# Pair rows of six tiles read whole during the last four expert blocks, with a masked second gather for the late rows

## The chip, the cores and the metric

One core of a Trainium2 chip runs the kernel. The metric is the device time of one execution in microseconds. The kernel before took 610.31 us (median of three runs, 609.31 to 610.9).

## The reference, cut to what matters

One decoder layer over 1024 prompt tokens and 64 sample tokens of width 1024. Four mixers and an output projection give `x`; the part around the change is the mixture of experts and the last norm:

```
expert(token)   = the two best of 8 experts in the best of 4 groups      # 32 experts, F = 128
out(token, k)   = silu(h @ w_gate[e_k]) * (h @ w_up[e_k]) @ w_down[e_k]  # k = 0, 1
x(token)        = x + gate_0 * out(token, 0) + gate_1 * out(token, 1)
y(token)        = rmsnorm(x, g_final)
```

## The kernel before, in words

**Tiles and blocks.** The 1088 tokens make nine tiles: 0 to 7 of 128 tokens, tile 8 of 64. After the router the work goes by blocks: a block is up to 128 (token, choice) pairs of one expert, or 64 and 64 of two experts with few rows (a pair block). `NB` is 29, so the blocks are 0 to 28; blocks 0 to 7 serve experts 0 to 7, blocks 8 to 18 are mostly pair blocks and the second halves of large experts, and blocks 19 to 28 serve one expert each, in an order that VectorE works out (`pos`, `order`). Blocks 25 to 28 serve the experts at places 28 to 31.

**A block on each engine.** GpSimd gathers the block's rows of `scratch_h` with an indirect DMA (line 1202). TensorE transposes them (`expert_T`, line 2364), multiplies by gate and up weights split in high and low parts (`expert_GU`, lines 2400 to 2402, or 2386 for pair blocks), transposes the activation (2411) and multiplies by the down weights (`expert_D`, 2425). ScalarE and VectorE each copy one half of the result into `outb`, which has two slots, so block b waits for the scatter of block b-2 (`expert_out`, lines 1006 and 1760). GpSimd then scatters the rows to `scratch_out` (line 1217), where row 2t+k is the output of choice k of token t. For all but pair blocks, `by_size` reads table entries first and issues for 32, 64, 96 or 128 rows.

**What orders the work around the change.** SyncE issues the loads of expert weights into eight slots: the 36 KB a partition at `o_x1` (`wfirst`) hold the weights of places 0, 1 and 2 modulo 8, those at `o_hT` (`wlater`) the other five. After its last weight load SyncE waits for `moe_done`, which GpSimd sets (`all_scattered`, line 1266) once every scatter has landed. Then SyncE reads all nine tiles of `scratch_out` into `opair`, 8 KB (both choices) a token, in the order `FINAL` = 8, 0, 1, 2, 3, 4, 7, 5, 6 (line 652), and behind them on the same queue it writes each finished tile out (line 498). Blocks beyond NB (overflow) run in loops guarded by `total`, a count of them.

**The final stage.** Tiles 0, 2, 4, 5, 6 are summed by TensorE (`own_rows`, line 2479, adds x by the identity; line 2496 adds the two choices by diagonal matrices `dg` of the gates), tiles 8, 1, 3, 7 by VectorE (`add_experts`, line 1961). ScalarE squares a tile with its sum and takes the root (lines 669, 1096, 1081). VectorE scales it (`final_norm`, lines 1969 and 1974). VectorE's own order is written out by hand:

```
add 8, norm 8, add 1, norm 0, norm 1, norm 2, add 3, add 7, norm 3, norm 4, norm 7, norm 5, norm 6
```

**Elsewhere.** `between` (line 1908) puts small VectorE work behind chosen blocks. During the input projection SyncE loads sixteen pieces of `w_in` in turn, two of them in flight (`load_piece`, line 505), each waiting for the use of an earlier one.

## Time and profile before

| | us |
|---|---|
| median of three runs (lowest, highest) | 610.31 (609.31, 610.9) |
| the profiled execution | 608.55 |
| its span, first to last instruction | 606.5 |
| TensorE busy in the span | 571.4 (94%) |
| VectorE busy | 439.9 (73%) |
| ScalarE busy | 242.2 (40%) |
| GpSimd busy | 88.5 (15%) |

The profiled execution took 2.05 us more than its span, for what lies around the first and the last instruction. "Busy" counts time in instructions of an engine; a wait is idle time, and the profile names what ended it. The mean granted clock of TensorE was 0.981 of full speed. A DMA shows two things: the time its issue took on the queue of the issuing engine, and the time from issue to landing.

### The profile page before, as it was taken

To read this page: it belongs to the slowest core of one execution; us is meant where nothing else is said; L and a number is where in the kernel's file an instruction comes from. 1 tells how busy PE (TensorE), PEld (TensorE's weight loads), DVE (VectorE), ACT (ScalarE), POOL (GpSimd) and SP (SyncE) were. 2 spreads that over 40 slices of the span, in tenths; PEclk is the share of its full clock that TensorE was granted. 3 is DMA by queue.
4 is the path that set the end of the run, shared out by engine and by line. 5 is a ranking of instruction groups with operands and counts; after the bars stand their busy time and mean duration, and the time that the engine had idled before them with its cause. 6 is when DMAs were issued, how large, how long until landed. Compare 5 with 4: busy or idle time off the path is not lost.

```text
span 606.5 us, 9765 instructions
## 1 busy us (share of the span) xinstructions
PE 571.4 (94%) x3401; PEld 473.4 (78%) x3401; DVE 439.9 (73%) x749; ACT 242.2 (40%) x389; POOL 88.5 (15%) x136
## 2 busy tenths in 40 slices
PE   8899999999999999899999995899997999999775
PEld 6799999997899889688888874777654768887222
DVE  4937997999999696746666658899731667786285
ACT  6642112222212427322222116576322567775443
POOL 4300000200000000100000000433331334431000
PEclk9999999999999999999999997899998999999889
DMA  8761210131112202455422107699989999962697
GB/s 317 150 123 38 69 36 1 36 93 35 36 36 79 105 36 69 114 203 198 157 80 93 54 36 247 215 332 404 392 329 412 407 352 395 394 241 97 209 421 299
DMA packets 52598, 111.27 MB, mean 183 GB/s; under 512 B 10867, under 2 KB 29176, under 8 KB 51449
## 3 DMA queue, kind: packets, MB, share of 16 engines
q1 hardware_dynamic: 44773, 92.18, 43.2%
q0 software_dynamic: 7168, 17.84, 8.2%
q8 instruction: 30, 0.49, 0.3%
q10 hardware_dynamic: 596, 0.50, 0.3%
q14 instruction: 31, 0.25, 0.1%
HBM read 96.36 MB, written 21.86 MB: 195 GB/s over the span
## 4 chain that ended last, share of the span: by engine, by line
PE 51%; DVE 17%; DMA 7%; issue 3%; ACT 2%; SPq 1%; POOL 0%; POOLq 0%; DVEq 0%; ACTq 0%
PE ps L2259 14%; PE ps L2081 9%; PE ps L2425 6%; PE ps L2364 3%; PE ps L2386 3%; PE ps L2400 3%; PE ps L2401 3%; PE ps L2402 3%; DMA at_opair_p<-scratch_out 3%; DMA at_wlater<-in_expert_w_down 3%; DVE at_mixP L1360 3%; PE ps L2496 2%; PE ps L2323 2%; DVE at_hT L1319 1%; DVE at_lnsq L1546 1%
## 5 line engine op out<-in xcount | busy, mean ns | idle before, releaser
L2081 PE MATMUL ps<-at_hT,at_ring 128*128 128x384 f32 x936 | 165.5, 333 | 0.0
L2081 PEld LDWEIGHTS ps<-at_hT,at_ring 128*128 128x128 f32 x936 | 155.9, 188 | 5.1 <-issue 5.0
L2259 PE MATMUL ps<-at_hT,at_mring 128*128 128x512 f32 (+1 forms) x432 | 102.7, 393 | 2.0 <-DVE at_mring L1514 1.3
L2259 PEld LDWEIGHTS ps<-at_hT,at_mring 128*128 128x128 f32 (+1 forms) x432 | 77.3, 182 | 21.3 <-DVE at_mring L1514 1.7
L1360 DVE SCALAR_TENSOR_TENSOR at_mixP<-at_uc,at_par,at_mixP 128x1024 f32<-128x1024 f32 x60 | 77.1, 1285 | 2.1
L2400 PE MATMUL ps<-at_whi,at_hTm 128*128 128x256 f32 x176 | 51.0, 290 | 0.0
L2402 PE MATMUL ps<-at_whi,at_hTm_lo 128*128 128x256 f32 x176 | 49.1, 279 | 0.0
L2364 PEld LDWEIGHTS ps<-sb_ident,at_xg 128*128 128x128 f32 x232 | 29.3, 192 | 18.2 <-issue 15.2
L1795 DVE TENSOR_TENSOR at_wlater_lo<-at_wlater,at_whi 128x1024 fp32r<-128x1024 f32 x30 | 36.7, 1225 | 6.0 <-ACT at_whi L988 5.1
L2425 PE MATMUL ps<-at_wlater,at_actT 128*128 128x512 f32 (+1 forms) x92 | 38.0, 597 | 0.7 <-ACT at_actT L1003 0.7
L988 ACT ACTIVATE at_whi<-at_wlater 128x1024 fp32r<-128x1024 f32 x30 | 31.6, 1055 | 7.3 <-PE ps L2402 6.5
L669 ACT ACTIVATE at_wk<-at_x 128x1024 f32<-128x1024 f32 (+1 forms) x13 | 13.8, 1059 | 51.4 <-DVE at_x L1586 44.8
L2364 PE MATMUL ps<-sb_ident,at_xg 128*128 128x128 f32 x232 | 31.6, 279 | 2.5 <-DMA at_xg<-scratch_h,at_gidxs 2.3
L1777 DVE TENSOR_TENSOR at_hTm_lo<-ps,at_hTm 128x1024 fp32r<-128x1024 f32 x21 | 25.7, 1223 | 11.2 <-ACT at_hTm L969 11.1
L2401 PE MATMUL ps<-at_wlater_lo,at_hTm 128*128 128x256 f32 x120 | 33.6, 280 | 0.0
L2400 PEld LDWEIGHTS ps<-at_whi,at_hTm 128*128 128x128 f32 x176 | 33.1, 188 | 0.2
L2402 PEld LDWEIGHTS ps<-at_whi,at_hTm_lo 128*128 128x128 f32 x176 | 33.0, 188 | 0.0
L1217 POOL DMA_INDIRECT scratch_out<-at_outb,at_sperm x21 | 20.8, 989 | 69.2 <-DVE at_outb L1765 69.2
L1202 POOL DMA_INDIRECT at_xg<-scratch_h,at_gperm x21 | 26.2, 1246 | 20.5 <-issue 14.4
L1765 DVE COPY at_outb<-ps 128x512 f32<-128x512 f32 x29 | 19.9, 686 | 10.6 <-PE ps L2425 10.5
L1012 ACT ACTIVATE at_outb<-ps 128x512 f32<-128x512 f32 x29 | 17.3, 597 | 25.5 <-PE ps L2425 23.2
L2127 PE MATMUL ps<-at_ring,at_hT 128*128 128x256 f32 (+1 forms) x216 | 25.9, 282 | 0.0
(324 smaller groups left out, 919.2 us busy)
## 6 DMA issues: line engine op xcount, KB each, us to landing
at_wlater<-in_expert_w_gate SPq DMA_DIRECT2D x20, 512.0 KB, 11.1
at_wlater<-in_expert_w_up SPq DMA_DIRECT2D x20, 512.0 KB, 12.8
at_wlater<-in_expert_w_down SPq DMA_DIRECT2D x20, 512.0 KB, 15.4
at_raw<-in_w_in SPq DMA_DIRECT2D x16, 512.0 KB, 4.0
at_opair_p<-scratch_out SPq DMA_DIRECT2D x8, 1024.0 KB, 14.7
at_wfirst<-in_expert_w_gate SPq DMA_DIRECT2D x12, 512.0 KB, 9.0
at_wfirst<-in_expert_w_up SPq DMA_DIRECT2D x12, 512.0 KB, 10.0
at_wfirst<-in_expert_w_down SPq DMA_DIRECT2D x12, 512.0 KB, 12.5
```

The costliest lines, as they stand in the source:

```text
L988: nc.scalar.activation(whi[h][:], half(wexp(w), h), ACT.Copy).then_inc(s[f"w_hi{h}"], 1)
L1202: g.indirect_dma_start(xg[0:n, b % XG, :], None, hs, bass.IndirectOffsetOnAxis(ap=index[0:n, :], axis=0), bounds_check=last_token, oob_is_ ...
L1360: do(stt(y, x, par[:, c, k:k + 1], y, ALU.mult, ALU.add))
L1795: v.tensor_tensor(half(wexp_lo(w), h), half(wexp(w), h), whi[h][:].bitcast(F32), ALU.subtract).then_inc(s[f"w_lo{h}"], 1)
L2081: mm = pe.matmul(ps[:, bank + r, 0:t1 - t0], w[:, wpart, k * P:(k + 1) * P], hT[:, hpart, k, t0:t1], start=(m, wpart, hpart) == (0, 0, 0), ...
L2127: mm = pe.matmul(b[0:n, 0:W].rearrange("p (s c) -> p s c", s=2), hT[:, hpart, k, i * P:i * P + n], vw[:, :, wpart, k * P:(k + 1) * P], sta ...
L2259: mm = pe.matmul(ps[0:n, b + r, :], mring[:, 1 - i % 2, mpart, k * P:k * P + n], wo[:, wpart, k, r * 512:(r + 1) * 512], start=(c, mpart, ...
L2364: mm = pe.transpose(rows_psum(b)[:, k // 4, k % 4 * P:(k % 4 + 1) * P], xg[:, j % XG, :].rearrange("p (q k) -> p k q", k=KC)[:, k, :], ide ...
L2400: pe.matmul(out, x, high, start=k == 0, stop=False)
L2401: pe.matmul(out, x, low, start=False, stop=False)
L2402: mm = pe.matmul(out, x_low, high, start=False, stop=k == KC - 1)
L2425: mm = pe.matmul(ps[n, bank + r, :], actT[:, j % 2, n], wexp(place(j, t or 0))[:, q:q + 512], start=True, stop=True)
```

## The change

SyncE copies rows of `x_prompt` and `x_sample` over the whole of `scratch_out` during the input projection (`fill_out`, ten DMAs), so that no row of it is unwritten. When the scatters up to block 24 have landed, SyncE reads tiles 8, 0, 1, 2, 3, 4 (`EARLY`) whole. The scatters of blocks 25 to 28 (`HELD` = 4) are held by GpSimd until these six reads have landed; for that, the results of blocks 26 and 27 go into buffers of their own (`kept`). After `moe_done`, SyncE reads only tiles 7, 5, 6 (`WHOLE`), and GpSimd gathers over the six early tiles, with six indirect DMAs, the 8 KB rows of those tokens that have an expert at place 28 or later; all other indices are out of bounds and are left out. VectorE works out the list of these tokens behind blocks 14, 15 and 16. The count of overflow blocks is now worked out on all partitions. `opair` and `dg` get other places. In the final stage the users of an early tile wait for its late gather too.

The diff, cut to its core:

```diff
 DVE_TILES = [8, 1, 3, 7]
+EARLY = [8, 0, 1, 2, 3, 4]
+WHOLE = [7, 5, 6]
...
-        opair_s = at("opair_s", [P, 2 * D], o_x1)
+        kept = [at("kept0", [P, D], o_x1 + 8 * D * 4), at("kept1", [P, D], o_hT + 8 * D * 4)]
+
+        def out_rows(r):
+
+            return kept[r - NB + 3][:] if NB - 3 <= r < NB - 1 else outb[:, r % 2, :]
+
+        def out_waits(eng, b, i, j):
+
+            if isinstance(b, int):
+                if 2 <= b < NB - 3:
+                    eng.wait_ge(scat[b % 2], 16 * (b // 2))
+                if b == NB - 1:
+                    eng.wait_ge(scat[b % 2], 16 * (b // 2 - 1))
+            else:
+                eng.wait_ge(scat[j % 2], 16 * (i * (LAP // 2) + j // 2))
+
...
 
         def opair(i):
-            return opair_s[:] if i == LAST else opair_p[:, i, :]
+            n = FINAL.index(i)
+            return opair_a[:, n, :] if n < 4 else opair_b[:, n - 4, :]
 
...
         actT = at("actT", [P, 2, P], o_sg + 2048)
-        ov = at("ov", [1, 2, NE], o_sg + 3072)
-        ovi = at("ovi", [1, NE], o_sg + 3328, I32)
-        ovm = at("ovm", [1, NE], o_sg + 3328)
-        again = at("again", [1, NE + 1], o_w + 14624)
+        ov = at("ov", [P, 2, NE], o_sg + 3072)
+        ovi = at("ovi", [P, NE], o_sg + 3328, I32)
...
         ovb = at("ovb", [1, 3, OVER], o_sg + 3456)
-        dg = at("dg", [P, len(PE_TILES), 2, P], o_x1 + 2 * D * 4)
+        dg = at("dg", [P, len(PE_TILES), 2, P], o_hT + (TILES - 4) * 2 * D * 4)
...
+            def fill_out(n):
+
+                r = n * 256 % NP
+                for src, at_, count in ((a["x_prompt"][0, r:r + 256, :], n * 256, 256),) if n < 8 else tuple(
+                        (a["x_sample"].rearrange("b t d -> (b t) d"), 2 * NP + h * NS, NS) for h in range(2)):
+                    sp.dma_start(orow[at_:at_ + count, :], src).then_inc(s["out_filled"], 16)
+
             for p in range(2, NPIECE):
                 load_piece(p)
+                if 5 <= p < 14:
+                    fill_out(p - 5)
...
+            def load_pairs(i):
+
+                n = rows(i)
+                src = orow[2 * i * P:2 * (i * P + n), :].rearrange("(t k) d -> t (k d)", k=2)
+                sp.dma_start(opair(i)[0:n, :], src).then_inc(pair_in[i], 16)
+
+            b = NB - HELD - 1
+            for k in range(2):
+                sp.wait_ge(scat[k], 16 * ((b + 2 - k) // 2))
+            for i in EARLY:
+                if i == EARLY[4]:
+                    sp.wait_ge(s["d_done"], b + 2)
+                load_pairs(i)
+
...
             sp.wait_ge(s["moe_done"], 1)
-            for i in FINAL:
-                n = rows(i)
-                src = orow[2 * i * P:2 * (i * P + n), :].rearrange("(t k) d -> t (k d)", k=2)
-                sp.dma_start(opair(i)[0:n, :], src).then_inc(pair_in[i], 16)
+            for i in WHOLE:
+                load_pairs(i)
...
-                if not (isinstance(b, int) and b < 2):
-                    act.wait_ge(scat[j % 2], 16 * (i * (LAP // 2) + j // 2))
-                nc.scalar.activation(outb[:, j % 2, 0:512], ps[:, bank, :], ACT.Copy)\
+                out_waits(act, b, i, j)
+                nc.scalar.activation(out_rows(j)[:, 0:512], ps[:, bank, :], ACT.Copy)\
...
-                                         outb[0:n, b % 2, :], None, bounds_check=last_pair,
+                                         out_rows(b)[0:n, :], None, bounds_check=last_pair,
                                          oob_is_err=False).then_inc(scat[b % 2], 16)
 
-                if is_pair(b):
+                if is_pair(b) or NB - 4 <= b < NB:
...
+            pool.wait_ge(s["out_filled"], 16 * 10)
...
+
+            pairs = orow.rearrange("(t k) d -> t (k d)", k=2)
+
+            def late_pairs():
+
+                pool.wait_ge(s["turns_ready"], 1)
+                for i in EARLY:
+                    g.indirect_dma_start(opair(i), None, pairs,
+                                         bass.IndirectOffsetOnAxis(ap=later[:, i:i + 1], axis=0),
+                                         bounds_check=last_token, oob_is_err=False).then_inc(pair_late[i], 16)
 
             for b in range(-XG, NB + 1):
                 n = b + XG
...
                     gather_over(n - NB)
+                if b == NB - HELD + 1:
+                    for i in EARLY:
+                        pool.wait_ge(pair_in[i], 16)
                 if b >= 1:
                     scatter(b - 1, columns(b - 1)[1])
 
...
                 all_scattered(NB)
+                late_pairs()
             over_from(0)
+            with pool.If(total > 0):
+                pool.wait_ge(s["moe_done"], 1)
+                late_pairs()
 
 
         @block.vector
...
+            do(v.memset(eidx[:], 0.0))
...
-                do(ts(ovi[:], carry[0:1, :], float(P - 1), None, ALU.add))
+                do(ts(ovi[:], carry[:], float(P - 1), None, ALU.add))
                 do(ts(ovi[:], ovi[:], 7, None, ALU.logical_shift_right))
...
-            between = {1: expert_order, 2: light_columns, 3: extra_columns, 4: other_columns,
+                do(v.tensor_copy(ovt[:, 2 * OVER:2 * OVER + 1], incl[0:1, NE - 1:NE]), s["ov_ready"])
+
+            def pair_turns():
+
+                do(v.memset(turn[:, 0:FIX], 0.0))
+                do(v.tensor_copy(turn[:, FIX:NE], pos))
+                shape = [P, TILES * 2, NE]
+                w = both[:].rearrange("p t k e -> p (t k) e")
+                chosen = eidx[:].rearrange("p t k -> p (t k)").unsqueeze(2).broadcast_to(shape)
+                do(tt(w, io32[:].unsqueeze(1).broadcast_to(shape), chosen, ALU.is_equal))
+                do(tt(w, w, turn[:].unsqueeze(1).broadcast_to(shape), ALU.mult))
+
+            def pair_latest():
+
+                do(v.tensor_reduce(latest[:], both[:], AX_X, ALU.add))
+                do(tt(done_by[:], latest[:, :, 0], latest[:, :, 1], ALU.max))
+                do(ts(no_over[:], incl[:, NE - 1:NE], 0.5, None, ALU.is_le))
+                do(ts(token[:], pid[:, :, 0], 0.5, -0.5, ALU.mult, ALU.add))
+
+            def pair_lists():
+
+                do(ts(done_by[:], done_by[:], place(NB - HELD) - FIX - 0.5, no_over[:], ALU.is_le, ALU.mult))
+                do(stt(later[:], done_by[:], float(NONE), token[:], ALU.mult, ALU.add), s["turns_ready"])
+
+            between = {14: pair_turns, 15: pair_latest, 16: pair_lists, 1: expert_order, 2: light_columns, 3: extra_columns, 4: other_columns,
                        6: overflow_counts, 7: overflow_sums, 8: overflow_lists, 9: overflow_experts,
...
+                if i in EARLY:
+                    dve.wait_ge(pair_late[i], 16)
...
                 pe.wait_ge(pair_in[i], 16)
+                if i in EARLY:
+                    pe.wait_ge(pair_late[i], 16)
...
```

## Rows read from the trace of the kernel before

**Rows 1.** The page: shares of the chain that ended last, by engine.
```profile
PE 51%; DVE 17%; DMA 7%; issue 3%; ACT 2%; SPq 1%; POOL 0%; POOLq 0%; DVEq 0%; ACTq 0%
```

**Rows 2.** The chain from 555 us on: start us, us, what.
```profile
560.50 4.02 DMA scratch_out<-at_outb,at_sperm
...
567.41 0.48 SPq L652
...
570.11 16.12 DMA at_opair_p<-scratch_out
...
586.28 5.40 PE ps L2496 x8
...
593.39 6.88 PE ps L2496 x16
...
602.10 1.28 DVE at_x L1974
```

**Rows 3.** VectorE's instructions in order of time, final stage: start us, us, what, idle before.
```profile
572.59 2.59 DVE L1961 SCALAR_TENSOR_TENSOR at_x<-at_opair_s,sb_gates,at_x 64x1024 f32<-64x1024 f32 x2 [4.51 <-DMA at_opair_s<-scratch_out]
576.86 0.15 DVE L1969 RECIPROCAL sb_rs<-sb_rs 64x1 f32<-64x1 f32 x1 [1.68 <-ACT sb_rs L1081]
...
587.12 5.25 DVE L1961 SCALAR_TENSOR_TENSOR at_x<-at_opair_p,sb_gates,at_x 128x1024 f32<-128x1024 f32 x4
592.40 0.16 DVE L1969 RECIPROCAL sb_rs<-sb_rs 128x1 f32<-128x1 f32 x1
...
593.92 0.16 DVE L1969 RECIPROCAL sb_rs<-sb_rs 128x1 f32<-128x1 f32 x1
```

**Rows 4.** Line 652's reads: issues; issue to landing of first, sixth and ninth.
```profile
L652 SPq DMA_DIRECT2D at_opair_p<-scratch_out x8: 422/432/583, 567.9 to 571.5; - x8
...
DMA to landing us min/median/max: 5.0/5.0/5.0
...
DMA to landing us min/median/max: 16.1/16.1/16.1
...
DMA to landing us min/median/max: 22.0/22.0/22.0
```

**Rows 5.** Engines by stretch: PE, PEld, DVE, ACT, POOL busy, granted clock, DMA share, GB/s.
```profile
571.00:572.00 1.00, 1.00 (x4) 0.49 (x3) 0.00 (x0) 0.92 (x3) 0.00 (x0) 1.00 1.04 238
...
588.00:590.00 2.00, 2.00 (x3) 0.66 (x2) 1.93 (x3) 0.18 (x1) 0.00 (x0) 0.50 1.04 434
```

**Rows 6.** GpSimd's instructions: scatters of blocks 24 and 28, and moe_done.
```profile
545.41 1.00 POOL L1217 DMA_INDIRECT scratch_out<-at_outb,at_sperm  x1 [4.58 <-DVE at_outb L1765]
...
563.34 0.92 POOL L1217 DMA_INDIRECT scratch_out<-at_outb,at_sperm  x1 [1.92 <-DVE at_outb L1765]
567.28 0.10 POOL L1270 MEMSET at_gcol<- 128x1 int32 x1 [3.03 <-DMA scratch_out<-at_outb,at_sperm]
```

**Rows 7.** Line 1217's scatters, issue to landing: blocks 24, 28 and 23.
```profile
DMA to landing us min/median/max: 3.6/3.6/3.6
...
DMA to landing us min/median/max: 3.9/3.9/3.9
...
DMA to landing us min/median/max: 5.4/5.4/5.4
```

**Rows 8.** GpSimd's third gather, behind its second: start us, us, idle before.
```profile
383.35 0.99 POOL L1202 DMA_INDIRECT at_xg<-scratch_h,at_gidxs  x1 [0.30 <-issue]
```

**Rows 9.** Line 1202's gathers, issue to landing: at 380.1 us, and at 525.0 us.
```profile
DMA to landing us min/median/max: 4.4/4.4/4.4
...
DMA to landing us min/median/max: 8.3/8.3/8.3
```

**Rows 10.** VectorE's instructions: one between-step of 608 elements, and idle time in block 15.
```profile
431.88 0.77 DVE L1886 TENSOR_TENSOR at_otmp<-at_ov,sb_iob 1x608 f32<-1x608 f32 x1
...
485.11 0.29 DVE L1757 TENSOR_TENSOR at_actv<-at_sg,ps 128x128 f32<-128x128 f32 x1 [2.45 <-ACT at_sg L995]
```

**Rows 11.** SyncE's queue during the input projection: ten pieces of w_in.
```profile
62.42 130.17 SPq L524 DMA_DIRECT2D at_raw<-in_w_in  x10
```

More of the change, by code:

```diff
@@ L59 @@
 DVE_TILES = [8, 1, 3, 7]
+EARLY = [8, 0, 1, 2, 3, 4]
+WHOLE = [7, 5, 6]
+HELD = 4
 NPAR = 31 + 3 + 4
@@ L294, in build_layer @@
         order = at("order", [P, 8, REST], o_state + 2304)
+        both = at("both", [P, TILES, 2, NE], o_state)
+        turn = at("turn", [P, NE], o_state + 2304)
+        latest = at("latest", [P, TILES, 2], o_state + 2304 + 192)
+        done_by = at("done_by", [P, TILES], o_state + 2304 + 288)
+        token = at("token", [P, TILES], o_state + 2304 + 384)
+        later = at("later", [P, TILES], o_state + 2304 + 672, I32)
+        no_over = at("no_over", [P, 1], o_state + 2304 + 736)
         eid = at("eid", [1, REST], o_state + 3072, I32)
@@ L374, in build_layer @@
         pair_in = [sem(f"pair_in{i}") for i in range(TILES)]
+        pair_late = {i: sem(f"pair_late{i}") for i in EARLY}
         def wait_piece(eng, p):
@@ L596, in expert_block @@
                     sp.wait_ge(s["d_done"], i * LAP + max(done_in(NE + j - LAP), NB + j - LAP) + 1)
+                    for t in EARLY:
+                        sp.wait_ge(pair_in[t], 16)
+                    if j == 2:
+                        sp.wait_ge(scat[(NB - 3) % 2], 16 * ((NB - 3) // 2 + 1))
+                    if j == 5:
+                        sp.wait_ge(scat[(NB - 2) % 2], 16 * ((NB - 2) // 2 + 1))
                 load_expert(i, j, e, first)
@@ L1762, in expert_out @@
                 dve.wait_ge(s["d_done"], b + 1)
-                if not (isinstance(b, int) and b < 2):
-                    dve.wait_ge(scat[j % 2], 16 * (i * (LAP // 2) + j // 2))
-                v.tensor_copy(outb[:, j % 2, 512:D], ps[:, bank + 1, :]).then_inc(s["ob_dve"], 1)
+                out_waits(dve, b, i, j)
+                v.tensor_copy(out_rows(j)[:, 512:D], ps[:, bank + 1, :]).then_inc(s["ob_dve"], 1)
             def expert_hT_lo(i, j):
@@ L1872, in overflow_counts @@
                 do(v.memset(again[:], 0.0))
-                do(ts(few[0:1, :], pos[0:1, :], LIGHT - 0.5, None, ALU.is_le))
-                do(stt(again[:, FIX:NE], rest[0:1, :], 64.0, few[0:1, :], ALU.is_gt, ALU.mult))
-                do(ts(few[0:1, :], pos[0:1, :], LIGHT + LARGE - 0.5, -1.0, ALU.is_ge, ALU.add))
-                do(stt(run[0:1, :], rest[0:1, :], P + 64.5, few[0:1, :], ALU.is_le, ALU.mult))
-                do(stt(few[0:1, :], pos[0:1, :], LIGHT - 0.5, run[0:1, :], ALU.is_ge, ALU.mult))
-                do(stt(n_e[:, FIX:NE], few[0:1, :], 1.0, n_e[:, FIX:NE], ALU.add, ALU.mult))
+                do(ts(few, pos, LIGHT - 0.5, None, ALU.is_le))
+                do(stt(again[:, FIX:NE], rest, 64.0, few, ALU.is_gt, ALU.mult))
+                do(ts(few, pos, LIGHT + LARGE - 0.5, -1.0, ALU.is_ge, ALU.add))
+                do(stt(run, rest, P + 64.5, few, ALU.is_le, ALU.mult))
+                do(stt(few, pos, LIGHT - 0.5, run, ALU.is_ge, ALU.mult))
+                do(stt(n_e[:, FIX:NE], few, 1.0, n_e[:, FIX:NE], ALU.add, ALU.mult))
                 do(tt(n_e, n_e, again[:, 0:NE], ALU.add))
-                do(v.tensor_tensor_scan(incl, ones[0:1, 0:NE], n_e, 0.0, ALU.mult, ALU.add))
+                do(v.tensor_tensor_scan(incl, ones[:, 0:NE], n_e, 0.0, ALU.mult, ALU.add))
                 do(tt(ovm[:], n_e, again[:, 1:NE + 1], ALU.add))
```

18 lines of the change are left out of this document (10 added, 8 removed).

## The prediction

> **What bounds the kernel now.** I read the page's chain first, then the chain of waits over the last 50 us, then each engine's instructions there. TensorE holds 51% of the chain [rows 1], so the blocks are bound by its matmuls; the change takes nothing from them. What it can shorten is the end. There the chain goes from the scatter of block 27 (560.50) through the last scatter to SyncE's first read at 567.41, from the sixth read (570.11, landed 16.12 later) to TensorE's sum of tile 4 at 586.28, through the sums of tiles 5 and 6, and ends in VectorE's last scaling at 602.10 [rows 2]. So reads count, but the reads aren't all: VectorE starts its first add at 572.59, when tile 8 is in, and is a serial list from then on. Its work is four adds, 2.59 for tile 8 and 2.62 for each of the others (5.25 for two), 10.4 us, and nine norms; two norms behind each other start 1.52 us apart, so 13.7; after the first add it waits 1.68 for ScalarE whatever comes [rows 3]. That is **25.8 us that no earlier read can shorten**. It took 603.38 - 572.59 = 30.8, so at most 5.0 us of waiting on data can be won.
>
> **The reads.** Tile 8 takes 5.0 us from issue, the sixth read (tile 4) 16.1, the ninth, issued at 571.5, 22.0 [rows 4]. With the issues at 567.41 and 570.11 [rows 2] the first six reads together take 567.41 to 586.2 = **18.8 us**; nothing stands in their way, as the output stores are issued behind the last of the reads. The stretches show a slow start (238 GB/s with the DMA engines at 1.04 of their time) before the steady rate (434 GB/s, other DMAs' bytes included) [rows 5].
>
> **The change, part by part.**
> - *When the early reads start.* The scatter of block 24 is issued at 545.41 [rows 6] and lands 3.6 later [rows 7]: 549.0. SyncE's other condition, block 25's products, gates only the fifth and sixth read, which are issued 2 us behind the first, and blocks are some 5.5 us apart. First read: 549.1.
> - *When they have landed.* 549.1 + 18.8 = 567.9. From below: tile 8 as before, 5.0, and five tiles at the spacing of the last three, (571.5 + 22.0 - 586.2)/3 = 2.43, give 17.2. Nothing that TensorE needs is loaded in this time, so beside the blocks the reads cost nothing; with that cover gone they would cost the weights' place in the queue.
> - *The held scatters.* GpSimd stands in a wait for all six reads. Behind it are the scatters of blocks 25 to 28, and behind those `moe_done`, the late gathers and SyncE's three reads. The blocks themselves aren't held, since blocks 26 and 27 have buffers of their own and block 28 needs only scatter 24. Before, scatter 28 was issued at 563.34. Now the first goes at 568.0 and each next one 1.3 later (0.99 for the instruction and 0.30 of issue between two of GpSimd's, [rows 8]; the table look-ups of `by_size` are gone for these four). Scatter 28: 568.0 + 3.9 = 571.9. Landing 3.9 as before [rows 7] = 575.8; at worst 5.4 as block 23's under traffic. SyncE starts its three reads at 576.0 instead of 567.41: **8.6 us later.**
> - *What is read afterwards.* Routing the reference's own inputs gives 371 pairs in the last four experts, 337 tokens, 222 of them in the early tiles. So 222 x 8 KB = 1.8 MB are gathered and three tiles = 3.1 MB read, against 8.9 MB. At one MB tile in 2.43 us, 1.05 MB / 2.43 us = 0.43 MB/us, the 3.9 MB that are saved are worth 9 us of DMA, but only the 5.0 us above can be cashed on VectorE.
> - *The late gathers.* Tile 8 could be added 5.2 us after SyncE's start; now it needs a gather, issued 0.3 after `moe_done`, 576.2. A gather on idle DMA engines landed in 4.4 us, one beside streaming loads in 8.3 [rows 9]. Here it starts together with the three reads, is a small one (21 rows), and the reads take some 2 us to come up to speed: I take 6.0, 582.2. The next five are issued 1.3 apart and land to about 589; tile 0 at 583.5, tile 2 at 586, tile 4 at 589.
> - *The final stage.* VectorE: first add 582.3, plus 25.8 = 608.1. TensorE: after its own rows it is idle longer than now. Its clock stood at 0.50 (1.2 of 2.4 GHz) at 588 to 590, after a wait of 2.3 us for tile 4 [rows 5], and that sum took 5.40 where two tiles at full clock take 6.88 [rows 2]. So tile 0: 583.6 + 5.4 = 589.0, tiles 2 and 4 at 3.44 each to 595.9, own rows of tile 6 1.7, tiles 5 and 6 to 604.5; ScalarE 1.5 and VectorE's last norm 1.5: 607.5. VectorE's list is the later by a little. Both end 4 to 5 us behind now. The last store follows its norm as before.
> - *Fill.* Ten copies, 8.9 MB, one behind each piece of `w_in`. Ten pieces stand over 130.17 us [rows 11], 13 us for each, so a copy of 1.05 MB (twice that to move, some 5 us at the rate above) is over before the next piece is issued. Nothing; without this cover up to 5 us for a piece. The last piece is issued near 192 and GpSimd's first gather, which now waits for the copies too, goes at 380 [rows 9], so that wait is met long before.
> - *VectorE's list of late tokens.* Two instructions of 576 elements and a reduction, 0.77 each by the row of 608 [rows 10], with eight small ones of about 0.2, as the reciprocals of [rows 3]: some 3.7 us over three blocks. The part behind block 14 is 1.9, into an idle time of 2.45 that follows it [rows 10]; those behind 15 and 16 are 1.4 and 0.4, the first beside a pair block, for which VectorE splits no weights. Nothing; without that cover 0.7 of one or the other. The counts on 128 partitions in place of one keep their lengths, and no wait is shorter for the two new buffers, since those copies waited for TensorE.
>
> **Sum.** 8.6 (reads after `moe_done` later) + 1.1 (first add 6.3 instead of 5.2 behind them) - 5.0 (waits on VectorE that go) = **+4.7 us**. The profiled execution took 608.55, which is 1.8 below the median, so this gives 613.3 for it and 615.0 for a median. Lower bound: reads 1.6 shorter, gather 4.4: +1.5. Upper: scatters landing in 5.4, tile 8's gather in 8.3, 0.7 on VectorE's blocks: +9.2. About 0.3%, 1.8 us, is what a measurement of this kernel can tell from no change.
>
> **Rivals.**
> - *B, the reads are quick.* The slow start [rows 5] may belong to what was just written by the last scatters and to TensorE's branches at that time, not to the reads. Then they take 1 us and 5.5 tiles at 2.43 = 14.4, everything moves 4.4 us forward: +0.3, 610.6, no change. It decides if the six reads land before 565. Against it: the share of DMA time was full while the rate was half, and the first read is the same 64-row tile 8.
>   The Trainium skill (DMA: Bandwidth & Descriptors, "Anatomy of one DMA") gives about 2.0 us and the bytes at 436 GB/s per DMA, for one issued from GpSimd; by it the six reads would take 15.2, an estimate, and the sum would be +1.1. The trace doesn't agree so far: 18.8 for these very reads [rows 2, 4].
> - *C, the end is bound by the transfer.* The last tile lands at 571.5 + 22.0 = 593.5 now, and 13.0 us later the span of 606.5 ends. After the change, 4.9 MB from 576.0 at 0.43 MB/us and 2 us of start would be in at 589.5. If the end kept its distance to the last landing, it would be 4.0 us earlier: 606.3, faster. For it: reads are the longest DMA piece of the chain [rows 2]. Against it: VectorE's 25.8 us. It decides only if the first add can start before 603.38 - 25.8 = 577.6, 1.6 us after `moe_done`, which no gather does [rows 9].
> - *D, the late gathers crawl.* Beside three whole reads each lands in 8.3 or more, and GpSimd issues them 2 us apart. Tile 8 is in at 584.5, tile 4 at 576.2 + 10 + 8.3 = 594.5; TensorE then ends at 606.6. VectorE is later: 584.6 + 25.8 = 610.4, +7.0, 617.3; with slow scatters too, +8.5: 618.8. For it: in the stage of weight loads gathers take that long. Against it: 3.1 MB of reads are over after 9 us, and the gathers are small.
> - *E, it doesn't do what it says*: if an overflow block ran, everything would be gathered again. The trace shows `moe_done` 3.9 us behind the scatter of block 28 [rows 6], so none runs.
>
> **Chances.** Forecast (+1.8 to +7) 0.62, D 0.17, B 0.15, C 0.05, E 0.01. Slower: forecast, D and E, 0.80. Same: B, less a little of it that turns out faster, 0.14. Faster: 0.06. The range takes the forecast, most of D and the upper half of B: 610.8 to 619.0; C, the rest of B and the top of D are left out, under 0.2.
>
> **What would show it.** In the profile after: the six reads issued near 549 and the scatter of block 25 at 568 (before 565: B); scatters 1.3 apart; `moe_done` near 576; the first gathered tile added near 582; VectorE with almost no wait from there on (waits of over 3 us in all: C's or D's kind of end); TensorE's clock at half for tile 0. The block stage should end where it does; if TensorE's last product moves by over 1 us, the fill or the list behind blocks 14 to 16 was mispriced. The prediction is wrong if `moe_done` comes before 573 or VectorE's list after it takes much less than 25.8.

## The result and the profile after

The kernel before took 610.19 us (median of 4 runs), the changed one **622.41 us** (4 runs, 621.07 to 623.51): 2.00% slower, interval 1.75% to 2.25%. The forecast was 615.0, range 610.8 to 619.0: slower as expected, but by 12.2 us and not by 4.7. The profiled execution took 623.51 us, its span 621.3 (before: 608.55 and 606.5).

The page of the changed kernel, shares of the chain that ended last: TensorE 50, VectorE up from 17 to 20, DMA down from 7 to 3, and issue up from 3 to 6 [rows 1]:

```profile
PE 50%; DVE 20%; issue 6%; DMA 3%; ACT 2%; SPq 0%; POOL 0%; POOLq 0%; DVEq 0%; ACTq 0%
```

GpSimd's instructions in order of time (start us, us, what, idle before and what ended it), to be held against [rows 6]:

```profile
548.36 1.00 POOL L1271 DMA_INDIRECT scratch_out<-at_outb,at_sperm  x1 [4.59 <-DVE at_outb L1837]
571.58 0.98 POOL L1271 DMA_INDIRECT scratch_out<-at_outb,at_sperm  x1 [22.22 <-DMA at_opair_b<-scratch_out]
572.87 0.98 POOL L1271 DMA_INDIRECT scratch_out<-at_kept,at_sperm  x1 [0.30 <-issue]
...
575.43 0.98 POOL L1271 DMA_INDIRECT scratch_out<-at_outb,at_sperm  x1 [0.30 <-issue]
579.27 0.10 POOL L1338 MEMSET at_gcol<- 128x1 int32 x1 [2.86 <-DMA scratch_out<-at_outb,at_sperm]
579.53 1.05 POOL L1309 DMA_INDIRECT at_opair_a<-scratch_out,at_later  x1
580.88 1.00 POOL L1309 DMA_INDIRECT at_opair_a<-scratch_out,at_later  x1 [0.31 <-issue]
```

The first four lines are the hold: GpSimd stands 22.22 us in front of the scatter of block 25, then issues the four scatters 1.3 apart. `moe_done` follows at 579.27, and the first two late gathers (tiles 8 and 0) right behind. How long these six gathers and the nine whole reads took, by line; the first line in each pair is the form, the second issue to landing (min/median/max over all of them):

```profile
L1309 POOL DMA_INDIRECT at_opair_a<-scratch_out,at_later x4: 987/999/1049, 579.5 to 583.5; - x4
DMA to landing us min/median/max: 8.5/9.9/11.2
...
L685 SPq DMA_DIRECT2D at_opair_b<-scratch_out x5: 329/432/544, 553.9 to 580.2; - x5
L685 SPq DMA_DIRECT2D at_opair_a<-scratch_out x4: 424/465/580, 551.8 to 553.4; - x4
DMA to landing us min/median/max: 5.1/10.2/16.1
```

Tile 8's gather is the 8.5, tile 0's the 11.2. The sixth early read, issued at 554.5, is the 16.1. TensorE and VectorE from there on:

```profile
571.15 8.56 PE L2575 MATMUL ps<-at_x,sb_ident 128*128 128x512 f32 x16 [6.38 <-issue]
592.18 9.98 PE L2594 MATMUL ps<-at_opair_a,at_dg 128*128 128x512 f32 x16 [12.47 <-issue]
601.99 3.60 PE L2594 MATMUL ps<-at_opair_b,at_dg 128*128 128x512 f32 x8
...
607.14 7.03 PE L2594 MATMUL ps<-at_opair_b,at_dg 128*128 128x512 f32 x16
```

```profile
564.81 0.69 DVE L1837 COPY at_outb<-ps 128x512 f32<-128x512 f32 x1 [2.15 <-PE ps L2521]
...
588.14 2.59 DVE L2057 SCALAR_TENSOR_TENSOR at_x<-at_opair_a,sb_gates,at_x 64x1024 f32<-64x1024 f32 x2 [17.61 <-DMA at_opair_a<-scratch_out,at_later]
...
593.91 2.61 DVE L2057 SCALAR_TENSOR_TENSOR at_x<-at_opair_a,sb_gates,at_x 128x1024 f32<-128x1024 f32 x2
600.36 0.16 DVE L2065 RECIPROCAL sb_rs<-sb_rs 128x1 f32<-128x1 f32 x1 [3.85 <-ACT sb_rs L1135]
...
603.79 0.16 DVE L2065 RECIPROCAL sb_rs<-sb_rs 128x1 f32<-128x1 f32 x1 [0.43 <-ACT sb_rs L1135]
...
616.86 1.28 DVE L2070 SCALAR_TENSOR_TENSOR at_x<-ps,sb_rs,sb_gain 128x1024 f32<-128x1024 f32 x1
```

TensorE idles 12.47 us until tile 0's gather lands (580.88 + 11.2 = 592.1), and then takes 9.98 us for the 16 products of tiles 0 and 2, where the last 16 take 7.03. The 3 us are lost in tile 0's sum alone: ScalarE can square tile 0 at 598.82, 6.6 us after the sum began, and tile 2 at 602.25, 3.4 later.

```profile
598.82 1.02 ACT L1150 ACTIVATE at_wk<-ps 128x1024 f32<-128x1024 f32 x1 [6.51 <-PE ps L2594]
```

VectorE pays with a wait of 3.85 for the norm of tile 0. By stretch (PE, PEld, DVE, ACT, POOL busy, granted clock, DMA share, GB/s), the clock stands at 0.50 there (it is back at 1.00 from 598 on), and the DMA engines are full for ten microseconds before:

```profile
582.00:592.00 10.00, 0.00 (x0) 0.00 (x0) 2.55 (x2) 1.15 (x2) 3.96 (x4) 0.62 1.00 410
588.00:590.00 2.00, 0.00 (x0) 0.00 (x0) 1.83 (x2) 0.00 (x0) 0.00 (x0) 0.50 0.99 402
...
594.00:596.00 2.00, 2.00 (x4) 0.95 (x3) 1.96 (x2) 0.00 (x0) 0.00 (x0) 0.50 0.48 107
```

**The difference in four pieces.** I cut each profile at the start of VectorE's last expert copy (block 28), at `moe_done`, at the first add, and at the end of the last norm. All in us; the experiments from below are in the same table.

| kernel | last copy | to `moe_done` | to first add | VectorE's list | copy to end |
|---|---|---|---|---|---|
| before | 561.86 | 5.42 | 5.31 | 30.79 | 41.5 |
| before, profiled again | 564.12 | 5.16 | 5.20 | 29.26 | 39.6 |
| **after** | 564.81 | **14.46** | **8.87** | **30.00** | **53.3** |
| whole reads behind gathers | 564.58 | 14.47 | 4.27 | 27.93 | 46.7 |
| no late gathers | 563.11 | 14.56 | 0.31 | 25.93 | 40.8 |
| TensorE kept running | 564.86 | 14.09 | 8.92 | 27.14 | 50.2 |
| gathers move no row | 563.17 | 14.51 | 8.49 | 27.83 | 50.8 |
| tile 8's gather halved | 562.92 | 14.51 | 8.96 | 29.87 | 53.3 |
| no hold | 567.99 | 7.53 | 9.86 | 28.64 | 46.0 |
| three early | 563.32 | 7.12 | 9.04 | 29.89 | 46.1 |
| three early, gathers first | 563.79 | 7.54 | 4.18 | 30.66 | 42.4 |
| three early, one gather first | 563.58 | 7.56 | 4.13 | 30.82 | 42.5 |
| no early tiles | 564.50 | 5.27 | 5.77 | 28.29 | 39.3 |
| no early tiles, no fill | 563.55 | 4.98 | 5.20 | 29.04 | 39.2 |
| last four direct | 565.11 | 5.13 | 6.19 | 27.99 | 39.3 |

Between the profiles of before and after: 9.04 + 3.56 - 0.79 = 11.8 us behind the last copy, and 2.95 ahead of it, 14.8 in all, the difference of the spans. Against the second profile of the kernel before, the same pieces are 9.30, 3.67 and +0.74, 13.7 behind the last copy; so the list's share depends by 1.5 us on which profile is taken as the base.

### The profile page after: what moved, and what is told of

The parts are those of the page before. It is cut to its first block, busy times and chain, and to the rows that moved or that the text cites. A ratio compares the mean times of both kernels' runs of the same rounds, so it can differ in the third digit from the quotient of the medians.

```text
span 621.3 us, 9757 instructions
## 1 busy us (share of the span) xinstructions
PE 573.8 (92%) x3401; PEld 476.6 (77%) x3401; DVE 443.2 (71%) x760; ACT 242.3 (39%) x389; POOL 95.8 (15%) x142
## 4 chain that ended last, share of the span: by engine, by line
PE 50%; DVE 20%; issue 6%; DMA 3%; ACT 2%; SPq 0%; POOL 0%; POOLq 0%; DVEq 0%; ACTq 0%
PE ps L2355 13%; PE ps L2177 8%; PE ps L2521 6%; PE ps L2482 3%; PE ps L2460 3%; PE ps L2497 3%; PE ps L2496 3%; PE ps L2498 3%; DVE at_mixP L1432 3%; DMA at_wlater<-in_expert_w_down 2%; PE ps L2419 2%; PE ps L2594 2%; DVE at_hT L1391 1%; PE ps L2575 1%; DVE at_x L2070 1%
## 5 line engine op out<-in xcount | busy, mean ns | idle before, releaser
L2460 PEld LDWEIGHTS ps<-sb_ident,at_xg 128*128 128x128 f32 x232 | 29.9, 193 | 18.7 <-issue 14.5
L1271 POOL DMA_INDIRECT scratch_out<-at_outb,at_sperm x19 | 19.0, 1000 | 78.7 <-DVE at_outb L1837 56.1
L2223 PEld LDWEIGHTS ps<-at_ring,at_hT 128*128 128x128 f32 (+1 forms) x216 | 25.8, 185 | 0.0
## 6 DMA issues: line engine op xcount, KB each, us to landing
at_opair_b<-scratch_out SPq DMA_DIRECT2D x5, 1024.0 KB, 11.5
```

The source lines that it names most:

```text
L2223: mm = pe.matmul(b[0:n, 0:W].rearrange("p (s c) -> p s c", s=2), hT[:, hpart, k, i * P:i * P + n], vw[:, :, wpart, k * P:(k + 1) * P], sta ...
L2460: mm = pe.transpose(rows_psum(b)[:, k // 4, k % 4 * P:(k % 4 + 1) * P], xg[:, j % XG, :].rearrange("p (q k) -> p k q", k=KC)[:, k, :], ide ...
```

## The experiments

Two theories stood after the first look. **G**: the end is set by the late gathers, which crawl beside the three whole reads, and by TensorE, which goes to half clock in the wait for them. **H**: it is the hold; whatever comes behind `moe_done` 9 us late ends 9 us late.

Ratios below are to the kernel before, run beside each group of experiments (its median there was 609.55 to 610.95 us), with a 95% interval. Every time of an engine or a DMA is from one profiled execution.

### The gathers: alone, gone, and with TensorE busy

In the first, SyncE waits for the six gathers before its three whole reads:

```
             sp.wait_ge(s["moe_done"], 1)
+            for i in EARLY:
+                sp.wait_ge(pair_late[i], 16)
             for i in WHOLE:
                 load_pairs(i)
```

> The changed kernel with one more wait: SyncE issues the three whole reads (tiles 7, 5, 6) only when the six late gathers have landed. Theory (the gathers are slow because they share the DMA engines with the 3.1 MB of whole reads): tile 8's gather lands 4.4 to 5 us after its issue instead of 8.5, tile 0's in 5 to 6 instead of 11.2, the first add comes 4 us earlier, TensorE's first sum 6 earlier, and VectorE's list ends about 8 us earlier: some 614.5 us. Rival (masked gathers of 8 KB rows are slow by themselves): landings stay at 8.5 to 11 and the whole reads come later: 624 us or more.

Measured: 615.93 us, ratio 1.0101 [1.0068, 1.0134], 6.5 us faster than the change. Its gathers by line, and TensorE's first sum in order of time:

```profile
L1311 POOL DMA_INDIRECT at_opair_a<-scratch_out,at_later x4: 991/1000/1045, 579.3 to 583.3; - x4
DMA to landing us min/median/max: 3.9/4.9/5.2
```

```profile
585.50 9.76 PE L2596 MATMUL ps<-at_opair_a,at_dg 128*128 128x512 f32 x16 [6.05 <-issue]
```

The very same six gathers land in 3.9 to 5.2 instead of 8.5 to 11.2. The first add comes 4.6 us earlier behind `moe_done`, though the whole reads start 11 us later. They don't bind: VectorE needs tiles 7, 5 and 6 last. The clock is at half here too (0.50 from 584 to 590), after 6.05 of waiting.

In the second the gathers are replaced by six memsets of one column each, so the rows of late experts of the early tiles are left out of their sums:

```
                 for i in EARLY:
-                    g.indirect_dma_start(opair(i), None, pairs, ...)
+                    g.memset(scol[:, i:i + 1], 0).then_inc(pair_late[i], 16)
```

> The changed kernel without the six late gathers: six small memsets set their semaphores instead. It leaves out the gathering of the late rows, so early tiles are summed from what was read early. Theory (of the 12.2 us lost, the hold of the scatters takes 8.6 and the wait for gathers with what follows from it the rest, less the waits won): the first add comes at moe_done + 0.3 instead of + 8.9, TensorE sums tile 0 at once and at full clock, VectorE's list takes 25.8 to 27: some 610 us, as the kernel before, 12 below the changed one. Rival (the gathers cost little, the hold is all): 617 us or more.

Measured: 609.94 us, 1.0006 [0.9987, 1.0026]. VectorE's first add and last norm, then TensorE's first sums:

```profile
577.98 2.59 DVE L2055 SCALAR_TENSOR_TENSOR at_x<-at_opair_a,sb_gates,at_x 64x1024 f32<-64x1024 f32 x2 [9.32 <-POOL at_scol L1309]
...
602.62 1.29 DVE L2068 SCALAR_TENSOR_TENSOR at_x<-ps,sb_rs,sb_gain 128x1024 f32<-128x1024 f32 x1
```

```profile
579.14 7.03 PE L2592 MATMUL ps<-at_opair_a,at_dg 128*128 128x512 f32 x16
```

With nothing to gather the whole hold of 9.1 us (14.56 against 5.42) is won back, and nothing more: 5.0 by the first add, which follows `moe_done` at once, and 4.9 by the list, which shrinks from 30.79 to **25.93**. H by itself would leave this kernel at 619. The 12.5 us between this kernel and the change are what the gathers cost as they were put.

The third keeps TensorE busy in its wait with twelve products that are written over later:

```
+            for n in range(12):
+                pe.matmul(sum_banks(0)[:, n % 2, :], ident[:],
+                          x1[:, 0, n % 2 * 512:(n % 2 + 1) * 512], start=True, stop=True)
             for t in (0, 2, 3):
                 own_rows(t)
```

> The changed kernel, and TensorE multiplies an identity by tile 0's rows twelve times (some 11 us of work whose product is written over) in its idle time ahead of its own rows, so that it idles for about 1 us and not for 12.5 before the first sum. If VectorE's waits in the final stage come from TensorE's first two sums at half clock (9.98 us for 16 products where 7.03 is a full-clock row), the sums of tiles 0 and 2 take 7.0 to 7.5, VectorE's wait of 3.85 shrinks to 1 or less and the time is 618.5 to 620. If the waits come from the late landing of tile 0's and tile 2's gathers alone, the sums start as late as before and the time stays at 622.4 +-1.

Measured: 620.07 us, 1.0167 [1.0127, 1.0208]. TensorE, VectorE's wait for tile 0, and the stretch that was at 0.50:

```profile
574.75 11.64 PE L2582 MATMUL ps<-at_x,sb_ident 128*128 128x512 f32 x24
586.23 5.31 PE L2575 MATMUL ps<-at_x,sb_ident 128*128 128x512 f32 x12
591.91 7.11 PE L2597 MATMUL ps<-at_opair_a,at_dg 128*128 128x512 f32 x16 [0.36 <-issue]
```

```profile
597.22 0.16 DVE L2065 RECIPROCAL sb_rs<-sb_rs 128x1 f32<-128x1 f32 x1 [0.98 <-ACT sb_rs L1135]
```

```profile
594.00:596.00 2.00, 2.00 (x6) 0.91 (x5) 1.96 (x2) 0.32 (x1) 0.00 (x0) 1.00 0.59 131
```

The sums start at the same time as in the change (591.91 against 592.18) and take 7.11 instead of 9.98, tile 0's 3.8 instead of 6.6 (ScalarE starts on it at 595.68); VectorE's wait falls from 3.85 to 0.98, its list from 30.00 to 27.14. So the half clock was worth 2.9 us of the list, and the landing alone the 1.4 of waits that stay. The rows say it first: in the sums TensorE is at 1.2 GHz after 12.47 idle, and at 2.4 GHz when it has worked since 571. The work didn't help at once: from 568 to 576 the clock stood at 0.50 in this run too, behind a wait of 6.36, though TensorE was busy from 572 on. The Trainium skill (TensorE: Matmul & The Clock Gate, "Part 1: The HAM clock gate") states that an idle engine is throttled and that activity releases it; the trace agrees.

### Bytes, packets or neither

Why do the gathers crawl? Two runs for that. In the first all six are issued as before, but every index is masked, so that no row moves (the late rows are left out of the sums again):

```
-                do(ts(done_by[:], done_by[:], place(NB - HELD) - FIX - 0.5, ...))
+                do(ts(done_by[:], done_by[:], 1000.0, ...))
```

> The changed kernel with every row of the six late gathers masked: the same six instructions of 128 indices, issued at the same times, but none moves a row (the late rows of the early tiles are left out of their sums). In the profile of the change these gathers are 864 packets, 642 to 690 of them below 512 B, and 1.82 MB. If the bytes make them slow beside the whole reads, they now land in 3 to 5 us, tile 0's first sum starts 6 to 7 us earlier behind moe_done, and the time is 613 to 616. If it is the number of packets, each of which takes its turn behind a large packet of a read, the count stays at 864 and they still land in 7 us or more; the time is then 619 to 622.

Measured: 620.39 us, 1.0166 [1.011, 1.0221]. The DMA queues in a stretch of 23 us that holds the gathers and the three reads (queue, kind: packets, MB, share of 16 engines; q0 is GpSimd's), the six landings, and TensorE's first sum:

```profile
q1 hardware_dynamic: 656, 3.93, 46.3%
q0 software_dynamic: 873, 0.01, 2.2%
```

```profile
DMA to landing us min/median/max: 4.7/7.5/9.1
```

```profile
588.53 9.48 PE L2594 MATMUL ps<-at_opair_a,at_dg 128*128 128x512 f32 x16 [10.45 <-issue]
```

For comparison, q0 in the kernel with the whole reads behind the gathers, where it moved the real rows, in a stretch of 12 us (so the shares can't be compared):

```profile
q0 software_dynamic: 864, 1.82, 52.6%
```

A masked index isn't free: with no row moved there are as many packets as with 222 (the nine more lie in the first 0.7 us of the longer stretch). And the bytes aren't what makes a gather late. Tile 8's lands in 8.1 (8.5 with its rows), tile 0's in 9.1 (11.2). The further ones take less and less, 8.0, 6.9, 5.8, 4.7, so that the last five land within 1 us of each other, at 588.4 to 589.2, just when the last whole read is in (9.4 after its issue at 578.7); tile 8's was in at 586.0. The bytes are worth 2.1 us of tile 0's landing and 2.2 us of the list, the reads beside it the rest.

In the second only tile 8's gather is changed, to 64 indices in place of 128:

```
-                    g.indirect_dma_start(opair(i), None, pairs,
-                                         bass.IndirectOffsetOnAxis(ap=later[:, i:i + 1], axis=0),
+                    g.indirect_dma_start(opair(i)[0:rows(i), :], None, pairs,
+                                         bass.IndirectOffsetOnAxis(ap=later[0:rows(i), i:i + 1], axis=0),
```

> The changed kernel, with tile 8's late gather on 64 indices in place of 128 (tile 8 has 64 tokens; the other 64 indices were masked). By bytes nothing changes: the same 21 rows, landing 8.5 +-0.3, 622.4 +-1. If the number of packets sets the landing, tile 8's gather is 64 packets fewer (864 becomes 800) and lands 1.5 to 4 us sooner, and the first add comes that much earlier; but the list then waits for tile 0, so that the end gains 1.5 at most.

Measured: 621.98 us, 1.0186 [1.013, 1.0241]. Its six landings, of which tile 8's is the shortest:

```profile
DMA to landing us min/median/max: 8.6/11.2/11.6
```

8.6, as before: the number of the gather's own packets doesn't set it either (the other five took 0.4 to 1.8 longer than in the change, so nothing came of it elsewhere). What is left is a delay that any gather meets while reads of 1 MB are in the queues. What it consists of stays open; that fewer gathers in all would land sooner is not borne out by the kernel with three early tiles below, whose three gathers took 8.7, 11.1 and 12.9.

### The hold

The six early tiles are read from a second tensor in which nothing is ever scattered, beside the last scatters, and nobody holds; the copies use the two old buffers, the reads start once block 25's products are done (550.92), and the late gathers wait for them. What the early tiles sum is then not what the experts gave, except for the late rows.

```
-                src = orow[2 * i * P:2 * (i * P + n), :]...
+                src = (orow2 if i in EARLY else orow)[2 * i * P:2 * (i * P + n), :]...
...
-                if b == NB - HELD + 1:
-                    for i in EARLY:
-                        pool.wait_ge(pair_in[i], 16)
```

> The changed kernel without the hold: the early reads take their data from a second scratch tensor, to which the fill goes, so that GpSimd need not wait for them before it scatters blocks 25 to 28; they start when block 25's products are done. The buffers of blocks 26 and 27 are the old two slots. The early tiles so hold wrong rows for tokens that aren't gathered late. Theory (the hold costs what moe_done moves): moe_done within 2 us of the kernel before's place against TensorE's last product, the late gathers then wait for the reads to land, about as long as before moe_done; 8 us below the changed kernel: 613 to 616. Rival (the hold is hidden behind the DMA work that has to be done anyway): under 3 us gained, over 619.

Measured: 619.17 us, 1.0151 [1.0118, 1.0184]: only 3.2 us faster than the change. I had expected 613 to 616. VectorE's copies of blocks 27 and 28, then GpSimd's last scatter and `moe_done`, then the scatter of block 25 by line:

```profile
563.36 0.69 DVE L1834 COPY at_outb<-ps 128x512 f32<-128x512 f32 x1 [3.34 <-DMA scratch_out<-at_outb,at_sperm]
567.99 0.69 DVE L1834 COPY at_outb<-ps 128x512 f32<-128x512 f32 x1 [3.93 <-PE ps L2518]
```

```profile
569.44 0.97 POOL L1269 DMA_INDIRECT scratch_out<-at_outb,at_sperm  x1 [3.65 <-DVE at_outb L1834]
575.52 0.10 POOL L1335 MEMSET at_gcol<- 128x1 int32 x1 [5.11 <-DMA scratch_out<-at_outb,at_sperm]
```

```profile
L1269 POOL DMA_INDIRECT scratch_out<-at_outb,at_sperm x1: 986/986/986, 553.1 to 553.1; - x1
...
DMA to landing us min/median/max: 10.2/10.2/10.2
```

The scatters now run beside the reads, and both pay for it: block 25's lands in 10.2 us where 3.6 to 5.4 were usual for the last blocks [rows 7], and the six reads take 22.4 (550.92 to 573.3) instead of 18.8. Block 27's copy waits 3.34 for its buffer. ScalarE's half of it waits likewise, and with it the activation that TensorE needs for block 28; TensorE idles 2.95, then runs that block's last products at 0.50 of its clock, and the last copy slips to 567.99. So `moe_done` comes at 575.5: 3.8 earlier than in the change, but 5.8 later than in the kernel with no early tiles (569.8). Of the 9 us that the hold costs, more than half comes back in another form, since reads and scatters under way together are each slower than alone. This run mixes two things, the traffic and the two old buffers; with buffers of their own the slip of the copies should be smaller. That was not tried.

### How many tiles are early

Three tiles are read early instead of six (`EARLY = FINAL[:3]`, `WHOLE = FINAL[3:]`), first as in the change, then with SyncE's wait for all three gathers, then for tile 8's gather alone:

```
-EARLY = [8, 0, 1, 2, 3, 4]
-WHOLE = [7, 5, 6]
+EARLY = FINAL[:3]
+WHOLE = FINAL[3:]
```

> The changed kernel with three early tiles (8, 0, 1) instead of six, and six whole reads afterwards. Theory: the early reads take 10.2 us instead of 18.8, so the held scatters go 7 to 8.5 us earlier, hardly later than they could without a hold; tile 8's gather still lands in 8.5 us beside the whole reads: 611 to 613. Rival (the bytes after moe_done decide): 4 MB more are read then, 9 us at 0.43 MB/us, which eats the gain: 620 or more.

Measured: 615.49 us, 1.0104 [1.0068, 1.0141], worse than I thought.

> Three early tiles (8, 0, 1), and the six whole reads only when the three late gathers have landed: both levers together. From the profile of three early tiles (moe_done 570.4, first gather issued at 570.7) and the gather's 3.8 us when it is alone: first add at 574.6 instead of 579.5, gathers in by 578.5, whole reads landing from 583.7 (tile 2) to 597.5 (tile 6), TensorE's last sum 601, last norm 604: 5 us below three early tiles alone, some 610, level with the kernel before. Rival (holding the whole reads back costs as much as it gives): 614 or more.

Measured: 612.34 us, 1.0027 [1.0006, 1.0047].

> Three early tiles, and the whole reads wait for tile 8's late gather alone. First add at 574.6 as with all gathers first; the reads start 4 us earlier than there, with the gathers of tiles 0 and 1 landing beside their slow start; tile 6 in at 594, VectorE's list of 25.8 and some 2 of waits from 574.6: ends at 602.5, 1 to 3 us below the kernel with all gathers first, 608 to 609. Rival (gathers of tiles 0 and 1 land as late as beside whole reads in the changed kernel, 11 us, and hold TensorE): 612 or more.

Measured: 610.59 us, 0.9992 [0.9969, 1.0015], no gain where I had hoped for one; of all kernels with early tiles and every row in its sums this is the fastest. TensorE's first sum with three early tiles, then, with one gather first, SyncE's queue and TensorE's third sum (a sum of 8 products, after a wait for tile 4):

```profile
583.22 10.16 PE L2594 MATMUL ps<-at_opair_a,at_dg 128*128 128x512 f32 x16 [6.56 <-issue]
```

```profile
550.53 25.00 SPq L685 DMA_DIRECT2D at_opair_a<-scratch_out  x4
575.59 4.08 SPq L685 DMA_DIRECT2D at_opair_b<-scratch_out  x5
```

```profile
589.00 5.38 PE L2595 MATMUL ps<-at_opair_b,at_dg 128*128 128x512 f32 x8 [2.23 <-DMA at_opair_b<-scratch_out]
```

The hold shrinks as it should: `moe_done` comes 7.1 to 7.6 behind the last copy instead of 14.5. In the first the gathers crawl as before (8.7 to 12.9 to land), so the first add is still 9.04 behind. Once a gather has the DMA engines to itself the first add is 4.1 behind, 1.1 better than in the kernel before. But then six whole tiles are left to read from 575.2 on, and the list is the 30.8 of the kernel before: the same kind of wait for tile 4 and the same half clock behind it. In this last kernel tile 0's gather, issued 2.4 us ahead of the first read, landed in 4.8, and tile 1's, issued 1.1 ahead, in 8.1. So there is a bill on both sides: few early tiles leave the reads at the end, many put a hold of up to 9 us ahead of them.

### What costs nothing, and what the kernel before does by itself

All early tiles taken out, with the hold and the two extra result buffers, the rest of the change kept (fill, lists of late tokens, counts on 128 partitions, direct scatters of the last four blocks, pair buffers in their new places); then the fill out as well:

```
-EARLY = [8, 0, 1, 2, 3, 4]
-WHOLE = [7, 5, 6]
+EARLY = []
+WHOLE = FINAL
```

> The changed kernel with no early tile at all: no early reads, no hold, no late gathers, the old two slots for the results; all nine tiles are read after moe_done. What is left of the change is the fill, VectorE's list behind blocks 14 to 16, the counts on all partitions, and scatters of blocks 25 to 28 without table look-ups. Theory (the block stage ended 1.3 to 2.9 us later in five profiles, all from the scatters of blocks 10 to 12, where weights are waited for; the side work causes that): 611.5 to 613. Rival (that stall moves by itself, or the early reads cause it): 610 within 0.5.

Measured: 608.47 us, 0.9971 [0.995, 0.9992].

> As the one with no early tile, and without the fill. If the fill's 8.9 MB of copies disturb the block stage (scratch memory or DMA order), this is 1 to 2 us below that one, at 610. If the counts on 128 partitions or the list do it, it is level with that one. If neither, both are at 610.

Measured: 608.82 us, 0.9969 [0.9948, 0.999]. With or without fill the same, and neither slower than before: fill, lists and counts cost nothing, as forecast. Both are 0.3% faster than the kernel before, by little more than the interval. To see whether the direct scatters do that, the kernel before with these alone:

```
-                if is_pair(b):
+                if is_pair(b) or NB - 4 <= b < NB:
                     move(P)
```

> The kernel before with one thing of the change: the scatters of the last four blocks always move 128 rows, without the choice by size from a register. Nothing is filled, held, read early or gathered late. If the 0.3% that the kernels without early tiles won comes from these scatters following faster upon the last copy, this gives 608.0 to 609.0 (ratio 0.997 +-0.002) with the end of the scatters 0.4 to 0.7 us earlier behind the last copy than before. If it came from the new places of the pair buffers (tile 8 beside the others), this gives 610.2 +-0.5, no difference.

Measured: 609.68 us, 0.9986 [0.996, 1.0013]. `moe_done` is 5.13 behind the last copy, as in the two profiles of before (5.42, 5.16), so the look-ups that are gone gave nothing there. Where the 0.3% comes from stays open; the new places of the pair buffers are left as a candidate, untested.

Last, the kernel before unchanged, profiled again:

> The kernel before, unchanged, profiled once more. Of the 14.8 us between the spans of the profiles of before and after, 2.95 lie in the blocks ahead of the change (the last copy of block 28 ends at 561.9 in the one and 564.8 in the other). If that is variation between executions, this profile of the very same code puts the last copy of block 28 somewhere in 561.5 to 565, and its time from that copy to the span's end stays at 44.6 +-0.7. If the fill or the lists caused it, the last copy is at 561.9 +-0.3 again.

Measured: 608.83 us, a single run. Its last copy, VectorE's row; under it the waits of TensorE in the block stage (line waited for: us in total, times, longest), of this profile, then of the first one:

```profile
564.12 0.69 DVE L1765 COPY at_outb<-ps 128x512 f32<-128x512 f32 x1 [2.15 <-PE ps L2425]
```

```profile
PE ps L2386 <- DMA at_wlater<-in_expert_w_down: 3.2, 1, 3.2
```

```profile
PE ps L2386 <- DMA at_wfirst<-in_expert_w_down: 2.5, 1, 2.5
...
PE ps L2386 <- DMA at_wlater<-in_expert_w_down: 0.6, 1, 0.6
```

The same code has its last copy at 561.86 in one execution and at 564.12 in the next, with the end nearly where it was (606.5 and 606.9). The tail moves as well: I had expected 44.6 +-0.7 from that copy to the end, and it is 42.8, mostly by a list of 29.26 in place of 30.79; TensorE's sum of tile 4 took 3.70 here after a wait of 2.41, not 5.40. In the blocks TensorE waits once or twice for weights, and not in the same place. The scatter of block 12, for one, is issued at 477.10 and at 479.36. So of the 2.95 us by which the changed profile is late at its last copy, 2.3 lie within what the kernel before does by itself, and the kernel with no early tiles shows 2.6. By the prediction's own sign (TensorE's last product moving by over 1 us) the fill or the lists were mispriced; that sign was a false alarm.

## Why the prediction was wrong

**Its direction and its first half held.** Term by term:

- *Early reads*: forecast 18.8 us from the first read; measured 551.8 to 554.5 + 16.1 = 570.6, again 18.8. Rival B (quick reads) fell with it, and so did the estimate of 15.2 by the Trainium skill's formula (DMA: Bandwidth & Descriptors, "Anatomy of one DMA").
- *The held scatters*: forecast 0.1 us after the last read, measured 1.0 (570.6 to 571.58), then 1.3 apart, and 3.84 from the last to `moe_done`. `moe_done` later by 8.6 in the forecast, 9.04 by the profiles.
- *Fill, lists, counts*: forecast nothing; nothing.
- *The late gathers*: **here the working failed.** Tile 8's gather was taken as 6.0, for being small and for the slow start of the reads; it took 8.5. The row that the forecast had for a gather beside streaming loads, 8.3 [rows 9], was the right one, and "the gathers are small" was no reason against it: with no row moved at all it still took 8.1. Tile 0 was to land 7.5 behind `moe_done` (583.5 against 576.0); it landed 12.8 behind (592.1 against 579.3). The first add is 8.87 behind `moe_done` where 6.3 was expected: the term of +1.1 measures **+3.56**.
- *The final stage*: the forecast cashed all 5.0 us of VectorE's waits; it got **0.79**. It had tile 0's sum start 1.3 us behind the first add and take 5.4; by its own numbers that left VectorE no wait for the norm of tile 0, but only 0.2 us to spare (590.5 against 590.7). The sum started 4.0 behind the first add (592.18 against 588.14), because tile 0's gather took 11.2 where tile 8's took 8.5, and lasted 6.6, at half clock after 12.47 idle, so VectorE waited 3.85 + 0.43. That tile 0's sum would be at half clock was foreseen; how late it would start was not. The run with TensorE kept running shows what the 4.2 over the minimum come to at full clock: 1.3 stay, 2.9 go. That the minimum itself, 25.8, was right is shown by the run without gathers (25.93).

Together +0.4, +2.5 and +4.2 over the forecast, 7.1; with the 4.7 that gives 11.8, against 12.2 by the medians.

**The rivals.** D was the right mechanism and its tile 8 (8.3) was right too, but it let TensorE keep up: "VectorE is later". It priced the first add and stopped there. Add the 4.2 of the list to its 617.3 and it would have said 621.5. C fell as argued; E did too, no overflow block ran.

**A point on the base.** The 5.0 us that "can be won" came from one execution of the kernel before. Profiled again it waits 3.5 (29.26 - 25.8), and three near relatives of it (no early tiles, without fill, last four direct) 2.2 to 3.2. A gather that has the DMA engines to itself brings the first add about 1 us forward besides (4.1 to 4.3 behind `moe_done`). So even with such a gather, and no wait left on VectorE, the prize was some 4.5 to 6 us, against a hold of 9; the forecast's own 8.6 and 5.0 say as much.

## What to carry to other kernels

A small transfer that opens the next stage should not be issued together with large ones that close it: order them, and let the big one wait for the small one (6.5 us here). Price it by the slowest row of its kind in the trace, and then go on to the engine behind it, since a longer wait there can also cost that engine its clock. Work pulled forward by holding other work back must be paid out of the DMA time that both use: 18.8 us of reads had to fit between two scatters, and without the hold more than half of the delay came back, with scatters of 9.4 and 10.2 us.

## What the runs showed of the hardware

- **A gather suffers far more from whole reads than they do from it.** Six gathers: 3.9 to 5.2 us alone, 8.5 to 11.2 beside three 1 MB reads. The three reads: 5.0, 7.1 and 9.9 alone, 5.1, 7.9 and 11.5 beside the gathers. I had expected a small transfer to slip through; even empty ones take up to 9.1. The Trainium skill (DMA: Bandwidth & Descriptors, "Queues, rings and completion order") says that each DMA engine takes turns between the queues that have work, a packet at a time. That would fit with bytes mattering little, but no run here shows the turns, and with 64 packets fewer tile 8's gather landed no sooner.
- **A masked row is still a packet**: 873 packets in GpSimd's queue with 0.01 MB and all rows masked, 864 with 1.82 MB and 222 rows.
- **Scatters suffer alike**: 10.2 and 9.4 us beside the early reads, 3.6 to 5.4 in the kernel before [rows 7]. That kernel has a slow one too, ahead of those: block 22's, issued at 534.30, took 8.5 while weights were still coming in (the last of them landed 22.2 us after its issue at 522.08, at 544.3).
- **TensorE falls to 1.2 GHz in waits of 5.99 to 12.47 us**, in each of the six profiles that have one before tile 0's sum and no work put into it, and the sums of tiles 0 and 2 then cost 9.48 to 10.16 instead of 7.03. After short waits it goes either way: a sum of one tile (3.70 at full clock) took 5.40, 5.38 and 5.18 after waits of 2.32, 2.23 and 2.45 us, and 3.70 after waits of 2.41, 2.44 and 2.27. A forecast from one such row has 1.7 us of luck in it.
- **The block stage has a jitter of 2 to 3 us** in the same code, with waits for weights that fall on different blocks. Differences between two profiles ahead of the changed place should be held against a second profile of the kernel before.
